# The rounding of the second z weight block moved ahead of the last tanh, its rest split between VectorE and GpSimd

## What is computed

```python
proj = u @ w_in[l]
q, k, v, z, xbc, dt_raw, g_a, g_b = _split(proj, IN_WIDTHS)
...
xbc = jax.nn.silu(causal_dwconv(xbc, conv_w, conv_b))
...
cb = jnp.einsum('bclgn,bcsgn->bgcls', cm, bm)
y_diag = jnp.einsum('bgjcls,bcsgjp->bclgjp', cb[:, :, None] * lmat, xdt)
...
y = y_diag + y_off + x * d_skip.astype(f32).reshape(SSD_GROUPS, SSD_HPG)[:, :, None]
y = y.reshape(b, s, SSD_INNER) * jax.nn.silu(z.astype(f32))
```

## Time and profile before

| | |
|---|---|
| median of three runs | 1083.49 us |
| lowest, highest | 1082.47, 1083.94 us |
| profiled execution: its own time | 1083.09 us |
| its span in the trace | 1081.4 us |
| granted clock of PE, mean | 0.996 |
| PE busy | 1051.6 us, 97% |
| DVE busy | 649.9 us, 60% |
| ACT busy | 454.6 us, 42% |
| POOL busy | 130.7 us, 12% |

### The profile page before, as it was taken

The page is one execution under the profiler, slowest core; times in us unless marked ns, Lnnn a source line. Parts: engine busy times, 40 slices in busy tenths (PEclk is TensorE's granted clock), DMA queues, the critical chain, the costliest instruction groups (busy, mean ns, idle before and its releaser), DMA issues.

```text
span 1081.4 us, 13741 instructions
## 1 busy us (share of the span) xinstructions
PE 1051.6 (97%) x5295; PEld 883.5 (82%) x5295; DVE 649.9 (60%) x863; ACT 454.6 (42%) x714; POOL 130.7 (12%) x200
## 2 busy tenths in 40 slices
PE   6999999999999999999999999999999999999997
PEld 5987887888779877888888888788888888888886
DVE  6788777876776777842433233466666666651214
ACT  6465456536654565532321213363434444431112
POOL 7113300330043013200000003120000000000001
PEclk8999999999999999999999999999999999999999
DMA  6321132114202420233233343412423333333221
GB/s 190 116 68 30 40 118 68 30 40 122 82 12 62 134 78 2 78 98 97 78 117 97 97 162 130 136 40 78 113 81 110 84 107 87 104 96 111 82 75 78
DMA packets 108426, 95.39 MB, mean 88 GB/s; under 512 B 12175, under 2 KB 98523, under 8 KB 108379
## 3 DMA queue, kind: packets, MB, share of 16 engines
q1 hardware_dynamic: 108379, 94.74, 28.8%
HBM read 92.63 MB, written 2.10 MB: 88 GB/s over the span
## 4 chain that ended last, share of the span: by engine, by line
PE 91%; DVE 5%; ACT 2%; DMA 1%; issue 1%; POOL 0%; DVEq 0%; POOLq 0%; SPq 0%; ACTq 0%
PE ps L1197 18%; PE ps L1199 18%; PE ps L1198 18%; PE ps L1204 9%; PE ps L1206 9%; PE ps L1205 9%; PE ps L1416 3%; DVE wlo L797 1%; PE ps L1412 1%; PE ps L1364 1%; PE ps L1428 1%; PE ps L1437 1%; DVE conv L899 1%; DVE conv L908 1%; PE ps L1239 1%
## 5 line engine op out<-in xcount | busy, mean ns | idle before, releaser
L797 DVE TENSOR_TENSOR wlo<-raw,whi 128x2048 fp32r<-128x2048 f32 (+2 forms) x83 | 188.7, 2275 | 213.2 <-ACT whi L452 213.2
L1197 PE MATMUL ps<-uhi,whi 128*128 128x512 f32 x640 | 249.6, 390 | 0.0
L1199 PE MATMUL ps<-uhi,wlo 128*128 128x512 f32 x640 | 249.1, 389 | 0.0
L1198 PE MATMUL ps<-ulo,whi 128*128 128x512 f32 x640 | 249.0, 389 | 0.0
L452 ACT ACTIVATE whi<-raw 128x2048 fp32r<-128x2048 f32 (+2 forms) x83 | 155.2, 1871 | 173.4 <-PE ps L1206 93.0
L1199 PEld LDWEIGHTS ps<-uhi,wlo 128*128 128x128 f32 x640 | 120.1, 188 | 25.0
L1197 PEld LDWEIGHTS ps<-uhi,whi 128*128 128x128 f32 x640 | 120.1, 188 | 24.8 <-DVE wlo L797 0.2
L1198 PEld LDWEIGHTS ps<-ulo,whi 128*128 128x128 f32 x640 | 120.1, 188 | 24.7
L1204 PE MATMUL ps<-whi,uhi 128*128 128x512 f32 (+2 forms) x320 | 122.2, 382 | 9.9 <-DVE wlo L797 9.9
L1206 PE MATMUL ps<-wlo,uhi 128*128 128x512 f32 (+2 forms) x320 | 119.3, 373 | 0.0
L1205 PE MATMUL ps<-whi,ulo 128*128 128x512 f32 (+2 forms) x320 | 119.2, 373 | 0.0
(11 more groups left out here) (220 smaller groups left out, 1437.7 us busy)
## 6 DMA issues: line engine op xcount, KB each, us to landing
raw<-in_w_in_dram SPq DMA_DIRECT2D x24, 1024.0 KB
raw<-in_w_up_dram SPq DMA_DIRECT2D x44, 512.0 KB
raw<-in_w_down_dram SPq DMA_DIRECT2D x11, 1024.0 KB
raw<-in_w_in_dram SPq DMA_DIRECT2D x16, 512.0 KB
raw<-in_w_ssd_out_dram SPq DMA_DIRECT2D x8, 1024.0 KB
raw<-in_w_attn_out_dram SPq DMA_DIRECT2D x4, 1024.0 KB
raw<-in_w_out_dram SPq DMA_DIRECT2D x4, 1024.0 KB
yT<-in_x_dram SPq DMA_DIRECT2D x4, 512.0 KB, 5.2
```

Of the source, the lines that this page charges most:

```text
L797: dve.tensor_tensor(wlo[sl][:, 0:width] if into is None else into, raw[sl][:, 0:width], h.bitcast(F32), ALU.subtract).then_inc(s["lo_done" ...
L1197: pe.matmul(bank(b)[:, span], hi_[:, k, c], ah[:, span], start=first and k == 0, stop=False)
L1198: pe.matmul(bank(b)[:, span], hi_[:, k, c], al[:, span], start=False, stop=False)
L1199: ins = pe.matmul(bank(b)[:, span], lo_[:, k, c], ah[:, span], start=False, stop=last and k == KD - 1)
```

## The change

ACT rounds block 6 (`hi_next(5)`) right behind tok(0), ahead of tanh(5) and of tok(1). The rest is made in two halves of 128 x 1024: DVE makes the first between silu(4) and silu(5), POOL the second between build(0) and build(1). A new semaphore, `zlo2_ok`, tells that POOL's half is there: PE waits for it ahead of the second half of z, in all four tiles, and SP ahead of loading the next block into the same buffer.

```diff
@@ sync: put
                 if n >= 2:
                     sp.wait_ge(s["lo_done"], n - 1)
+                if n <= N_C1 + 1 and n % PER_G == 1 and n > 1:
+                    sp.wait_ge(s["zlo2_ok"], n // PER_G)
@@ gpsimd: group
                 build(0)
+                sl = (G * PER_G + 6) % 2
+                pool.wait_ge(s["hi_done"], G * PER_G + 7)
+                pool.tensor_tensor(wlo[sl][:, BLK // 2:], raw[sl][:, BLK // 2:], whi[sl][:, BLK // 2:].bitcast(F32),
+                                   ALU.subtract).then_inc(s["zlo2_ok"], 1)
@@ scalar: group
                 tanh(4)
                 tok(0)
+                hi_next(5)
+                tanh(5)
                 act.wait_ge(s["xd_ok"], G * NT)
                 tok(1)
-                tanh(5)
...
                     if t == 0:
-                        hi_next(5)
                         tok(2)
@@ vector: group
                 silu(4)
+                lo_next(5, BLK // 2)
                 silu(5)
...
                         mask_decays(range(2))
-                        lo_next(5)
@@ tensor: z_tile
                             sl = block_ready(5 + h)
+                            if h:
+                                pe.wait_ge(s["zlo2_ok"], G + 1)
```

More of the change, by code:

```diff
@@ L158, in hybrid_block @@
             "x_in0", "x_in1", "x_in2", "x_in3", "consts_in", "par_in", "par2_in", "posT_ok", "pool_c", "loaded0", "loaded1", "hi_done", "lo_done", "blk_done",
-            "band_zero", "dve_chain", "pool_chain", "xsq", "rstd", "xn", "xT_mm", "u_plain", "uhi_ok", "u_ok", "u2_ok", "parT_mm", "par_ok",
+            "band_zero", "dve_chain", "pool_chain", "xsq", "rstd", "xn", "xT_mm", "zlo2_ok", "u_plain", "uhi_ok", "u_ok", "u2_ok", "parT_mm", "par_ok",
             "ang_ok", "rope_tab", "hp_ok",
```

## The result

The changed kernel takes 1094.95 us (median of 4 runs, 1093.8 to 1096.93) against 1083.03 for the kernel before beside it: a ratio of 1.0111, 95% interval 1.0094 to 1.0129. It is 11.9 us slower. The forecast was 1091.0, with a range that ended at 1093.0: the direction was right, the size was not, and the measured time lies above the range.

What follows compares the result with a forecast made beforehand. PE, busy 1051.6 of 1081.4 us, was taken as the bound. Four groups at 1.88 us, 7.5 us, on the profiled 1083.09 gave 1090.6; 0.4 for the higher median made it 1091.0, range 1084.1 to 1093.0.

Steps and rivals of the forecast that it cites:

- The two chains that meet at PE: At y_diag of tile 0, z and xdt arrive almost together; xdt only 0.2 us ahead, so freeing z needs xdt earlier too.
- ScalarE's part at nothing: On ACT, rounding moves to 181.49, delaying tanh(5), tok(1) and the exps; costed at nothing, at worst 0.3 us.
- Turns between DVE and POOL: Instructions of both engines that read SBUF run one after the other, alternating; POOL's 2.54 us and DVE's work add up.
- The sum of the chain, 1.88 per group: DVE's memset moves from 188.75 to 190.63, so y_diag starts 1.88 us later per group, 7.5 us in four.
- the price of POOL's half: POOL's 128x1024 subtraction taken as 2.54 us, from rows of the same subtraction on 512 elements.
- PE's stalls: In tile 0 of each group, PE waits about 1.5 us ahead of tok(4) and 2.3 ahead of y_diag, none at z.
- The step that failed: From PE's stalls to the time: y_diag's 1.88 us delay per group carried through unchanged, as PE has no later slack.

Runs made afterwards that it cites:

- The zeros: Changed kernel with POOL writing zeros into its half of the rest instead of subtracting, against the kernel before: 1083.09 us, ratio 1.0004.
- the split alone: Kernel before with only the rest split: DVE's half behind the masks, POOL's behind build(1), ACT's rounding not moved: 1090.91 us, ratio 1.0067.
- the filled version: Changed kernel plus eight matmuls that feed nothing, in PE's stall ahead of y_diag in each group: 1087.84 us, ratio 1.0046 to the kernel before.
- POOL's quarter: Changed kernel with POOL making a quarter of the rest and DVE three quarters: 1091.92 us, ratio 1.0088 to the kernel before.

## Why the prediction was right in direction and wrong in size

- **The two chains that meet at PE.** Right. Freeing z alone was worth nothing, since xdt ended only 0.2 us before PE began y_diag; the run with the whole rest on DVE shows it (ratio 0.9992). One row was misread on the way, without effect: the scores are four products, in the eight records of the earlier trace rows, not five.
- **ScalarE's part at nothing.** Right: the rounding ran from 184.88 - 3.40 = 181.48, and nobody waited for tok(1) or the exps. In the changed kernel:

```profile
184.88 1.92 ACT L458 ACTIVATE whi<-raw 128x2048 fp32r<-128x2048 f32 x1
```

- **Turns between DVE and POOL.** Right in every row, also who gets the turn when both wait, which I had from the earlier trace rows. The zeros and the split alone bear it out from both sides.
- **The sum of the chain, 1.88 per group.** Measured 1.63 at memset and 1.62 at the yardstick. Mis-sized was the price of POOL's half: I took 2.54 from two pieces of 512; where it first had to stand, it was done 2.35 behind the end of DVE's hold (190.29 - 187.94). That is 0.19 of the 0.25. Two other runs give the same price: 2.35 with the half behind build(1), 2.34 with the split alone.
- **PE's stalls**, 1.5 and 2.3 forecast: 1.35 and 2.08.
- **The step that failed** is the one from the stalls to the time. The sum took the later start of y_diag, 1.88 a group, as the whole cost, because what follows "hangs on it in both kernels". PE's pace behind the two forecast stalls it took as unchanged, a term put at nothing without a reason. But PE works on at half the clock behind such a stall, in three groups of the profiled run. This costs 6.4 us in the profiled run, as much as the whole chain, and filling the stall gives 7.1 back. The range, too, had bounds for turns and handovers but none for the clock; with the chain's 6.5 alone the time would have been inside it, as the 1087.8 of the filled version is.

The trace of before gave a false comfort: a PE stall of 1.98 us in each group, with a granted clock of 1.00 in the stretches behind it. In the changed kernel PE's stalls in tile 0 grew from 1.98 to 3.43 us, and the longer one moved. With 2.1 us ahead of the transposes one group of four was low; with 2.08 ahead of y_diag three, three and all four, and two in the run with POOL's quarter; with 3.1 us ahead of z three. The length alone does not decide: 1.25 us ahead of y_diag, the only long stall there in the run with zeros, was enough in two groups, and 1.98 ahead of z was not in any. What the place does, and what the light products of 64 columns do that come right behind it, is not separated.

Nor is a stall followed by a low stretch each time. Behind the groups every version has a stall of PE at the transposes of yT. In the five profiles in which it is 1.8 us or less, no low stretch follows it; in the seven in which it is 1.98 to 2.18, one follows in four. First the kernel before, then the one with the whole rest on DVE, each with the row of the stall and the stretch behind it:

```profile
703.76 1.09 PE L1214 MATMUL ps<-ident,yT 128*128 128x128 f32 x8 [2.03 <-ACT yT L715]
...
704.00:708.00 4.00, 4.00 (x26) 3.45 (x25) 2.51 (x3) 2.84 (x5) 1.48 (x4) 1.00 0.61 177
```

```profile
702.12 1.09 PE L1214 MATMUL ps<-ident,yT 128*128 128x128 f32 x8 [2.18 <-ACT yT L715]
...
703.00:707.00 4.00, 4.00 (x13) 3.13 (x12) 2.45 (x2) 2.54 (x6) 1.48 (x4) 0.57 0.80 226
```

So that the kernel before has no low stretch in its groups is known of one profiled execution only, and part of the difference between executions of one kernel may be of this kind. Why a given group is spared (group 1 in one trace of the changed kernel, group 2 in the next) stays open.

## What to carry to other kernels

Before an elementwise step is split between VectorE and GpSimd, look at what both read. Where both read from SBUF, as the halves here, they were made one after the other, and what was queued behind either engine paid too; VectorE's taps, with an input in PSUM, were not held up. Whether a split pays beside such instructions was not tried. Before a wait of PE is removed, look at what is due next and how late it is: here it was 0.2 us away. And a PE stall that is made longer or moved is to be priced at its length and, on top, at the risk of a low stretch behind it, 0.6 to 3.2 us here. Order the work so that the stalls stay short; here even useless matmuls in the stall made the kernel faster.

## What the runs showed of the hardware that was not expected

- PE's clock fell to half behind stalls of 2.08 us ahead of y_diag (two to four groups of four), 2.1 us ahead of the transposes (one of four), 1.25 us (two of four, in the run with zeros) and 3.1 us (three of four), and not behind 1.98 us at another place (none of four, in the one trace). Each low stretch costs 1.6 us here, the long one of group 0 3.2, and only 0.55 where PE would have waited behind it anyhow. The Trainium skill, page "TensorE: Matmul & The Clock Gate", section "What's actually happening", has a clock that is low by default and released by activity; this case's traces agree as to activity (0.50 behind the stall, 1.00 with it filled), and show nothing of a default.
- A POOL instruction that only writes (memset, 0.96 us) ran beside a VectorE subtraction with two SBUF inputs, which took the 1.22 us that it takes alone; the memset was done before it and so was not held. The Trainium skill, page "SBUF — State Buffer", section "SBUF: two separate sides", limits the exclusion of such a VectorE instruction to GpSimd instructions that read SBUF; this trace agrees.
- Where an instruction of each engine waited and both read SBUF, the turn passed to the other engine at each end, even though the next one of the same queue stood right behind: seg_lo and the masks, 1.49, 1.14, 1.49, 1.52 for instructions of 1.04 and 0.69.
